# Recurrence gates turned by TensorE instead of a round trip through memory, first convolution tap on ScalarE, norms cut in two

## The reference

```
xc  = causal_dwconv(xb, lru_conv_w) + lru_conv_b
r,i = sigmoid(xc @ w_a + b_a), sigmoid(xc @ w_x + b_x)      # by head of 256
a   = exp(-8 * r * softplus(-lam));  h_t = a_t*h_{t-1} + xc*i*sqrt(1-a^2)
y_b = h * silu(z_b)
x   = x + concat(y_a, y_b) @ w_out
```

## Time and profile before

| | |
|---|---|
| median of 3 runs | 3298.55 us |
| profiled execution, own time | 3297.41 us |
| its span, first to last instruction | 3295.6 us |
| PE busy | 3241.2 us (98%), 14,854 instructions |
| of them products L1752 to L1754 of blocks | 3 x 3136 + 3 x 1280 |
| DVE busy | 2184.4 us (66%) |
| ACT busy | 1676.3 us (51%) |
| POOL busy | 338.9 us (10%) |
| mean granted clock of PE | 0.995 |
| weights loaded | 512 KB a block, 4.0 to 5.6 us to landing |

### The profile page before, as it was taken

How to read it: one execution, slowest core, us unless ns; L and a number is a source line. 1 busy time by engine, 2 the same in 40 slices (tenths; PEclk the granted TensorE clock), 3 DMA queues, 4 the chain that set the end, 5 groups by cost and what they waited for, 6 DMA issues and landing times.

```text
span 3295.6 us, 39407 instructions
## 1 busy us (share of the span) xinstructions
PE 3241.2 (98%) x14854; PEld 2687.3 (82%) x14854; DVE 2184.4 (66%) x3066; ACT 1676.3 (51%) x2274; POOL 338.9 (10%) x541
## 2 busy tenths in 40 slices
PE   9999999999899999999899999999999999999999
PEld 7788888888788788887787888888888877888887
DVE  6558656766767766757667666766666677767664
ACT  5544444546654444456655554454545544555453
POOL 2000000001001000000100000111100333210000
PEclk9999999999999999999999999999999999999999
DMA  8676666576677566667676666666657655576665
GB/s 276 232 237 206 211 198 198 197 231 196 206 233 220 188 217 200 212 190 228 214 237 210 182 221 212 220 215 224 207 182 249 211 184 185 191 251 203 186 216 172
DMA packets 339822, 695.99 MB, mean 211 GB/s; under 512 B 26988, under 2 KB 29364, under 8 KB 339248
## 3 DMA queue, kind: packets, MB, share of 16 engines
q1 hardware_dynamic: 312608, 620.37, 59.1%
q0 software_dynamic: 24736, 66.79, 6.5%
q10 hardware_dynamic: 2288, 6.30, 0.5%
HBM read 647.42 MB, written 45.94 MB: 210 GB/s over the span
## 4 chain that ended last, share of the span: by engine, by line
PE 89%; DVE 4%; issue 3%; ACT 2%; DMA 1%; POOL 0%; ACTq 0%; DVEq 0%; SPq 0%; POOLq 0%
PE acc L1752 28%; PE acc L1754 28%; PE acc L1753 28%; DVE weights_lo L1280 1%; DVE work L1284 1%; PE nm L1938 1%; DMA kv_scratch<-work 1%; ACT work L997 1%; PE tr L1752 0%; PE tr L1754 0%; PE tr L1926 0%; PE tr L1753 0%; ACT weights_hi L986 0%; PE sc L1912 0%; PE tr L1828 0%
## 5 line engine op out<-in xcount | busy, mean ns | idle before, releaser
L1280 DVE TENSOR_TENSOR weights_lo<-weights_raw,weights_hi 128x1024 fp32r<-128x1024 f32 x1103 | 1340.2, 1226 | 842.2 <-ACT weights_hi L986 838.3
L986 ACT ACTIVATE weights_hi<-weights_raw 128x1024 fp32r<-128x1024 f32 x1103 | 1158.5, 1058 | 1176.5 <-PE acc L1754 1013.9
L1752 PE MATMUL acc<-weights_hi,u_hi 128*128 128x512 f32 x3136 | 1241.2, 396 | 25.9 <-DVE weights_lo L1280 25.9
L1754 PE MATMUL acc<-weights_hi,u_lo 128*128 128x512 f32 x3136 | 1225.1, 391 | 0.0
L1753 PE MATMUL acc<-weights_lo,u_hi 128*128 128x512 f32 x3136 | 1224.4, 390 | 0.0
L1752 PEld LDWEIGHTS acc<-weights_hi,u_hi 128*128 128x128 f32 x3136 | 591.0, 188 | 158.5 <-DVE weights_lo L1280 29.3
L1754 PEld LDWEIGHTS acc<-weights_hi,u_lo 128*128 128x128 f32 x3136 | 590.6, 188 | 124.7
L1753 PEld LDWEIGHTS acc<-weights_lo,u_hi 128*128 128x128 f32 x3136 | 591.1, 189 | 119.8
L1752 PE MATMUL acc<-weights_hi,y_hi 128*128 128x512 f32 x1280 | 502.3, 392 | 13.6 <-DVE y_lo L1595 10.5
L1754 PE MATMUL acc<-weights_hi,y_lo 128*128 128x512 f32 x1280 | 499.5, 390 | 0.0
L1753 PE MATMUL acc<-weights_lo,y_hi 128*128 128x512 f32 x1280 | 499.5, 390 | 0.0
(11 more groups left out here) (286 smaller groups left out, 1970.1 us busy)
## 6 DMA issues: line engine op xcount, KB each, us to landing
weights_raw<-in_w_in_dram SPq DMA_DIRECT2D x384, 512.0 KB, 4.0
weights_raw<-in_w_out_dram SPq DMA_DIRECT2D x256, 512.0 KB, 4.6
weights_raw<-in_a_w_in_dram SPq DMA_DIRECT2D x176, 512.0 KB, 4.5
weights_raw<-in_b_w_in_dram SPq DMA_DIRECT2D x112, 512.0 KB, 4.1
weights_raw<-in_c_w_in_dram SPq DMA_DIRECT2D x112, 512.0 KB, 4.4
weights_raw<-in_w_mem_kv_dram SPq DMA_DIRECT2D x63, 512.0 KB, 5.6
turn_scratch_uq<-work POOLq DMA_DIRECT2D x80, 128.0 KB, 3.0
work<-turn_scratch_uq SPq DMA_DIRECT2D x20, 512.0 KB, 5.5
```

The lines of the kernel that those rows point to most:

```text
L986: SC_E.activation(WH[:, b % RING], RAW[:, b % RING], ACT.Copy).then_inc(sem("hi_done"), 1)
L1280: V.tensor_tensor(WL[:, b % RING], RAW[:, b % RING], WH[:, b % RING].bitcast(F32), ALU.subtract).then_inc(sem("lo_done"), 1)
L1752: T.matmul(dst, hi_l, hi_r, start=start, stop=False, **kw)
L1754: return T.matmul(dst, lo_l, hi_r, start=False, stop=stop, **kw)
```

## The change

Five edits.

1. The gate `z_b` is turned by eight TensorE transposes into bank `tr` (piece `cz`, slot + 3) in place of flip, spill and fetch; `lrz` (+ 5) and `lry` (+ 7) read it there. Bank `tr` is free again at `lrz_y`. Lane `z` goes.
2. Tap 3 of every convolution is on ScalarE (with the bias where there is one); `conv` has three pieces, + 9, + 10 and + 11, with one tap each on VectorE, and what follows comes a slot later. `CVH` moves to another place of the work tile.
3. The gate rows go from slots 33 to 48 to slots 9 to 32.
4. Memory keys: flip at + 2, `qt` at + 8, + 12, + 12 and + 10.
5. `hn` is cut in `hn` and `hnw`, `fc` in `fc` and `fcw`, a slot apart. Attention starts a slot later, and the final gain is loaded ten slots earlier.

```diff
@@ Plan.chunk, Plan.pair
         e = self.piece(self.here(), kind, chunk=c, **kw)
+        if kind == "hn":
+            self.piece(self.here() + 1, "hnw", at=e)
@@ BANKS
+    "cz": {"tr": "lrz_y"},
@@ keys_in, memory keys
-        q = turn(pl.here() + 1, "n", ("hn_out", hn), "n")
-        q.twin = pl.piece(pl.here() + 8, "qt", at=q, buf="n", **kw)
+        q = turn(pl.here() + 2, "n", ("hn_out", hn), "n")
+        q.twin = pl.piece(pl.here() + after, "qt", at=q, buf="n", **kw)
-        keys_in(hn, gain=("par2", MK_ + i), dst="kt", store=("mk", i))
+        keys_in(hn, (8, 12, 12, 10)[i], gain=("par2", MK_ + i), dst="kt", store=("mk", i))
@@ queries and gate rows
-            for r in range(2):
+            for r in range(3):
                 pl.piece(pl.here() + 9 + r, "conv", to="cq", r=r, l=l, taps=QC + 4 * j)
-            pl.piece(pl.here() + 11, "cqs", j=j)
-        pl.piece(base + 33, "gates_w", ...)
-        g = pl.piece(base + 36, "gates_mm", xt=xt[3])
-        pl.piece(base + 39, "gates_in", g=g, l=l, two=True)
-        gate_rows(base + 40, True)
+            pl.piece(pl.here() + 12, "cqs", j=j)
+        pl.piece(base + 9, "gates_w", ...)
+        g = pl.piece(base + 12, "gates_mm", xt=xt[3])
+        pl.piece(base + 14, "gates_in", g=g, l=l, two=True)
+        pl.piece(base + 15, "gates_row", two=True)
+        pl.piece(base + 22, "gates_ser", two=True, r=0)
+        pl.piece(base + 23, "gates_ser", two=True, r=1)
+        pl.piece(base + 30, "gates_sum", two=True)
+        pl.piece(base + 32, "gates_exp")
@@ lru_in
-            c = pl.here() + 10
+            c = pl.here() + 11
-                pl.piece(pl.here() + 4 + 2 * w, "wax", w=w)
+                pl.piece(pl.here() + 6 + 2 * w, "wax", w=w)
             pl.piece(c + 1, "cvs")
             for w in range(2):
                 pl.piece(c + 3 + w, "lgate", l=l, p=p, w=w)
-            c += 2 * (p > 0)
+            c += p > 0
@@ lru_gate
-            q = turn(pl.here(), "xt", ("zb_out", zb), "z")
-            pl.piece(pl.here() + 8, "lrz", l=l, p=p, at=q)
-            lr.append(pl.piece(pl.here() + 10, "lry", l=l, p=p))
+            pl.piece(pl.here() + 3, "cz", at=zb)
+            pl.piece(pl.here() + 5, "lrz", l=l, p=p)
+            lr.append(pl.piece(pl.here() + 7, "lry", l=l, p=p))
@@ attention
             if late:
-                pl.piece(s, "fc")
+                fc = pl.piece(s + 1, "fc")
+                pl.piece(s + 2, "fcw", at=fc)
@@ ScalarE, new
+                    elif k == "conv" and p.r == 0:
+                        wait(act, "cj_out", last["cjoin"])
+                        for f in range(4):
+                            w = PAR[:, c + f:c + f + 1]
+                            if p.to == "cx":
+                                i = SC_E.activation(CV[:, f], XP[:, f, 3:259], ACT.Identity, scale=w, bias=PAR[:, b:b + 1])
+                            else:
+                                i = SC_E.activation(CV[:, f], XP[:, f, 3:259], ACT.Copy, scale=w)
+                        i.then_inc(sem("cv_t"), 1)
@@ VectorE, conv
+                        if p.r == 0:
+                            dve.wait_ge(sem("cv_t"), p.n // 3 + 1)
+                        tap = 2 - p.r
+                        for f in range(4):
+                            i = stt(CV[:, f], XP[:, f, tap:tap + 256], PAR[...], CV[:, f], ALU.mult, ALU.add)
@@ ScalarE and VectorE, lrz
-                        act.wait_ge(sem("fetched_xz"), 16 * (p.at.nth + 1))
-                        for t in range(2):
-                            i = tanh(tokens(ZT, t), by_token("z", t), scale=0.5)
+                        wait(act, "cz_pe", p)
+                        for j in range(2):
+                            i = tanh(ZT[:, 2 * j:2 * j + 2], TR[:, j]..., scale=0.5)
-                        for t in range(2):
-                            for f in range(4):
-                                i = stt(z, z, 1.0, by_token("z", t)[:, f], ALU.add, ALU.mult)
+                        for j in range(2):
+                            i = stt(z, z, 1.0, TR[:, j]..., ALU.add, ALU.mult)
@@ TensorE, new
+                    elif k == "cz":
+                        wait(pe, "zb_out", p.at)
+                        for j in range(4):
+                            for t in range(2):
+                                m = T.transpose(TR[:, j // 2, ...], XT[:, t, j * P:j * P + P], ID)
+                        m.then_inc(sem("cz_pe"), 1)
```

More of the change, by code:

```diff
@@ L127 @@
     "sv": {"sc": "sv_out", "nm": "sv_out"}, "params": {"tr": "par_out"}, "tbias": {"nm": "tb_out"},
-    "wst": {"tr": "ws_out", "t1": "ws_out"},
+    "wst": {"tr": "ws_out", "t1": "ws_out"}, "cz": {"tr": "lrz_y"},
 }
@@ L420, in queries @@
             else:
-                keys_in(hn, gain=gain, dst=dst, store=None)
+                keys_in(hn, 9, gain=gain, dst=dst, store=None)
         def attention(mode, grp, slot):
@@ L465, in make_plan @@
             gate(3)
-            tm = attention("mem", 3, pl.here() - NB + (4 if kind == "A" else 9))
+            tm = attention("mem", 3, pl.here() - NB + (4 if kind == "A" else 10))
             ts = []
@@ L498, in make_plan @@
                     pl.piece(h - 4, "spread_in", grp=grp)
-                ts.append(attention(kind, grp, h + 1 if grp < 2 else h - 3 if kind == "B" else h - 4))
+                ts.append(attention(kind, grp, h + 2 if grp < 2 else h - 3 if kind == "B" else h - 4))
         need = tiles([ts[0], ts[1], tm, ts[2]])
@@ L1112, in _ @@
                         wait(act, "flipped", last.get("flip"))
+                        wait(act, "cz_pe", last.get("cz"))
                         for t in range(2):
@@ L1176, in _ @@
                         wait(act, "cx_c", last["cx"])
-                        wait(act, "yb_lo", last.get("lry"))
+                        wait(act, "lw_pe", last.get("lgate"))
+                        wait(act, "mo_out", last["mo"])
                         if p.n == 0:
@@ L1237, in _ @@
                         wait(act, "gt_out", last.get("gt"))
-                        wait(act, "flipped", last.get(("flip", "z")))
+                        wait(act, "cz_pe", last.get("cz"))
                         for t in range(2):
@@ L1420, in _ @@
                     elif k == "conv":
[L1421 to L1441 removed]
+                        if p.r == 0:
+                            dve.wait_ge(sem("cv_t"), p.n // 3 + 1)
+                        tap = 2 - p.r
+                        c = p.l * NPAR + p.taps + 16 * tap
+                        for f in range(4):
+                            i = stt(CV[:, f], XP[:, f, tap:tap + 256], PAR[:, c + f:c + f + 1], CV[:, f], ALU.mult, ALU.add)
+                        if tap:
+                            step(i)
+                        else:
                             i.then_inc(sem(p.to + "_c"), 1)
```

53 lines of the change are left out of this document (22 added, 31 removed).

## The result

The changed kernel takes 3255.12 us (median of 4 runs, 3254.11 to 3258.12), the kernel before on the same chip 3298.07 (3294.63 to 3298.61): a ratio of 0.9873, interval 0.9856 to 0.9891, so faster by 43 us. The forecast was 3270. The time lies in the range (3250 to 3286) but outside the forecast's own range (3262 to 3279), and near the 3252 of rival A.

What follows compares the result with a forecast made beforehand. PE, busy 98% of the span, was taken as the bound. From 3298.55 us, -4.6 - 9.3 - 14.6 + 0.5 - 28.8 + 7.0 + 18.2 + 3.4 = -28.2 us gave 3270, range 3250 to 3286.

Steps and rivals of the forecast that it cites:

- rival A: Recurrence: the turned gate is ready in time, so 15.2 us and 3.4 us go: 3252; chance 0.22.
- Where time could go: Whole kernel: only PE's stops, its slower clock, or work added to or taken from PE matter; 60 us in reach.
- Memory keys, gate rows, block C: Stops there go: -4.6 us at the memory keys, -9.3 in the gate rows, -14.1 in block C.
- Transposes: Recurrence: PE gets 64 transposes; eight push the second product back 0.88 us each, +7.0 us.
- The new wait: Recurrence: PE's gate products wait until VectorE has used the turned gate in bank tr; 2.0 us in cycle one.
- the term for cycles two and three: Recurrence: late sqrt on ScalarE, scans and wa/wx parts delay VectorE's taps, making the wait 2.8 us each.
- The output chunk: Recurrence, after the last cycle: scans and lrz share slot 5, so the next split is 1.5 us late.
- Clock: Recurrence: half of the four 2.8 us stops lose 1.7 us to half clock, +3.4 us.
- B: Recurrence: a cover fails, the six stops are 4 us and all cost clock: about 3286; chance 0.18 with D.
- C: Recurrence: each of six stops becomes 5.3 us, with 3.4 us of clock lost: 3304; chance 0.05.
- D: Block C and gate rows: the moves do nothing, +9 or +14 us, 3279 or 3284; chance 0.18 with B.
- The tap: Convolutions: first tap to ScalarE at 2.08 us, priced at 0, bounds 0 and +8 us.

Runs made afterwards that it cites:

- Number 5: Changed kernel with memory keys, gate rows, uncut norms and attention start put back; recurrence, tap and turn of the keys stay as changed: 3282.84 us, ratio 0.9947.
- number 8: Changed kernel with only the norms of queries and heads in one piece again; attention stays one slot later: 3264.89 us, ratio 0.9909.
- number 7: Changed kernel with gate products of pieces after the first a slot later and the z gate turned by DMA at short distances: 3235.42 us, ratio 0.9807.
- number 2: Changed kernel with both gate products of pieces 1 to 3 one slot later: 3241.77 us, ratio 0.983.
- number 3: Changed kernel with a one-column tanh before ScalarE's wait for the convolution, loading the table in idle time: 3248.87 us, ratio 0.9853.
- Number 6: Changed kernel with the first tap of all sixteen convolutions back on VectorE: 3270.61 us, ratio 0.9912.
- number 1: Changed kernel with the z gate's transposes two slots earlier and its use three slots earlier for pieces 0 to 2: 3242.93 us, ratio 0.9833.
- number 4: Changed kernel with the z gate turned by VectorE and DMA at the old distances, as in the kernel before: 3263.15 us, ratio 0.9896.

## Why the prediction was right where it was, and wrong in the recurrence

**Where time could go.** Right: only stops, clock and work on PE moved the time. Blocks A and B, where PE's work only changed slots, sum to 0.0 us.

**Memory keys, gate rows, block C.** Right, within 0.9, 0.4 and 0.1 us. Number 5 brings each back in its own stage, the keys by 4.4 of 5.5. For the keys ScalarE's waits for the store were three, 17.7 us in all, and are one of 1.8, which PE doesn't feel. In block C the mechanism named (a split between each pair of steps) holds, but I put the shift of attention at nothing, and number 8 shows that the two shifts are some two fifths of the gain. I took two edits for one.

**Transposes.** Right. Predicted 0.88 us each, 7.0 in all; the second product behind them starts 1.10 us after the first transpose (731.31 to 732.41) where it would have been 0.23, and block by block number 7 against number 2 gives 0.90 each, 7.2.

**The new wait.** The mechanism, its place and its engine were right, and in cycle one also the size: I had the chain at 20.7 us and PE at 18.7, and both are within 0.2 of the trace; the wait is 1.75 for 2.0. The table load cost its 1.28, with tanh 0.02 us behind it, and number 3 took just about that off ScalarE.

**The step that failed** is the term for cycles two and three: "VectorE enters the taps 0.8 us later", 2.8 us each. ScalarE in cycle two:

```profile
772.87 1.06 ACT L993 ACTIVATE weights_hi<-weights_raw 128x1024 fp32r<-128x1024 f32 x1 [1.66 <-PE acc L1769]
773.84 1.25 ACT L1122 ACTIVATE work<-acc,smalls 128x512 f32<-128x512 f32 x2
...
777.92 2.07 ACT L1141 ACTIVATE work<-work,params_one 128x256 f32<-128x256 f32 x4
```

And VectorE's first tap there:

```profile
780.02 1.68 DVE L1308 SCALAR_TENSOR_TENSOR work<-work,params_one 128x256 f32<-128x256 f32 x4
```

The row to read is the idle 1.66 before the split: ScalarE had caught up and stood waiting for PE to free a buffer, so nothing of the last `lru` was left over. The tap begins 5.05 us after that split, in cycle one 5.04. A lag of the cycle before can't reach beyond such an idle. VectorE is another matter: before its tap in cycle one it stood idle for 0.56 us, and in cycle two not at all, since the scans and the two wa/wx parts did come in between. They used up those 0.56 us and no more: its tap begins 2.10 us after ScalarE's, in cycle one 2.11. All six waits are therefore alike, 10.6 us for 15.2.

**The output chunk:** 1.5 us predicted, 0.66 measured, twice; 1.7 us less. Which step of that estimate was too long was not traced.

**Clock.** I gave half of the four stops of 2.8 us a half clock, 3.4 us in all. None of 1.75 had any. Number 6, with stops of 2.5 and 3.06, lost it behind all six: had the stops been as long as I said, the term would have been twice mine. It was wrong because the stops were; that I had halved it kept the forecast nearer, by luck.

**Sum of the miss,** in us: 4.6 (waits) + 1.7 (output chunk) + 3.4 (clock) - 0.2 (transposes) + 2.4 (rest of the recurrence) = 11.9; memory keys, gate rows and block C 1.4; handover and start 1.7. Together 15.0 of 15.1. I put the rest of the recurrence and the keys' 0.9 down to a cost I didn't count: a stop takes more than its row says (below; 0.25 us a stop by number 1), and in the recurrence 20 stops became 8. The handover's stop was 1.98 us before, 1.49 in the changed kernel, and 1.16 to 1.98 in versions that edit nothing there; I don't put it down to the change, and its cause stays open.

**Rivals.** A's time was the nearest, but not its mechanism: the turned gate was not in time, and numbers 1 and 2 show what A really is worth, some 3242 us, 12 to 13 below. B and C are refuted (1.75 us, no clock), D as well (-9.7 and -14.2). **The tap,** priced at 0, was right for the query chunks; in the recurrence 15.5 us hang on it, and my price covered only its cost, not what it hides.

## What to carry to other kernels

When a cost is carried from one cycle to the next, look for an idle row of the engine in between: if it waits for the bottleneck there, the lag ends at it, and cycle two is cycle one. Ask of every moved piece not only what it costs where it goes but which chain it leaves: a 1.4 us step taken off VectorE in a chain that ends in a stop was worth 2.6 us at each of six stops here, 1.1 of wait and 1.5 of clock, since the stops of 1.75 us had no half clock behind them and those of 2.5 and 3.06 had. And after a new wait is found, try to shift either end of it by a slot or two before accepting it; the two ways gave 12 and 13 us.

## What the runs showed of the hardware

A stop costs more than its row. PE in the kernel before, around the first stop at the memory keys:

```profile
114.02 0.39 PE L1754 MATMUL acc<-weights_hi,y_lo 128*128 128x512 f32 x1
115.98 0.50 PE L1752 MATMUL acc<-weights_hi,y_hi 128*128 128x512 f32 x1 [1.57 <-DVE weights_lo L1280]
116.32 0.40 PE L1753 MATMUL acc<-weights_lo,y_hi 128*128 128x512 f32 x1
116.56 0.39 PE L1754 MATMUL acc<-weights_hi,y_lo 128*128 128x512 f32 x1
```

Products follow each other every 0.227 us but each is shown 0.39 long, so the idle of 1.57 is 1.96 - 0.23 = 1.73 of lost time; the next product starts 0.34 later instead of 0.23, and the block loses 1.87 in all. The three stops of the keys, 4.6 us of rows, are 5.5 us in the stages.

At which stops the clock fell to 1.2 GHz, over the traces of this case, PE's first instruction apart: at none up to 1.91 us; at both of 1.92 and 1.94 (number 5, each with a stop of 0.34 six us ahead); of the two of 1.98 at one (number 1) and not at the other (the kernel before, with two short stops ahead); at all from 2.01 us up (2.27, 2.51, 3.05, 3.12, 4.4, 5.3, 6.6). The half clock lasted 3.4 us in most cases and 6.8 at the longest. It began between 3.6 us before PE started again (within the stop of 6.6 in number 4) and 1.5 us after. The stretch in number 1, behind 1.98 us:

```profile
1722.40:1725.20 2.80, 2.80 (x8) 2.21 (x7) 2.43 (x3) 0.00 (x0) 0.00 (x0) 0.50 0.90 329
```

The same four-part tap costs VectorE 1.38 us as a tensor_scalar and 1.67 as a scalar_tensor_tensor, ScalarE 2.08: the slower engine was the better place, since it had the time.
